# Hybrid streaming encoder step, attention stage: a quarter of the full weight units split on GpSimd, causal mask on VectorE, reciprocals turned in 32 by 32 blocks, half of w_out split on GpSimd

## The reference

```python
s = jnp.einsum('bqhd,bkhd->bhqk', qi, k, preferred_element_type=jnp.float32) * sc
s = s + (Fi[:, :, :, None] - Ft[:, :, None, :])
s = jnp.where(kpos[None, :] <= qpos[:, None], s, -jnp.inf)
pr = jax.nn.softmax(s, axis=-1)
return jnp.einsum('bhqk,bkhd->bqhd', pr.astype(v.dtype), v)
...
z = jnp.concatenate([attn * jax.nn.silu(ag), pool * jax.nn.silu(pg)], axis=-1)
return x + gate[:, None, :] * (z @ w_out)
```

## Time and profile before

| | us |
|---|---|
| median of three runs | 1268.88 (1265.78 to 1271.44) |
| profiled execution, its time | 1271.73 |
| its span, first to last instruction | 1269.9 |
| mean granted TensorE clock | 0.989 of full speed |

### The profile page before, as it was taken

One profiled execution on the slowest core, in us unless ns is written; L12 is line 12 of the kernel. 1 busy time (PEld: TensorE's weight loads), 2 busy tenths in 40 slices (PEclk: granted clock), 3 DMA queues, 4 the chain that ended last, 5 costly groups with the idle time before them and its releaser, 6 DMA issues. The chain is left out here.

```text
span 1269.9 us, 19390 instructions
## 1 busy us (share of the span) xinstructions
PE 1231.5 (97%) x7023; PEld 1029.5 (81%) x7023; DVE 714.3 (56%) x1974; ACT 565.9 (45%) x1163; POOL 185.3 (15%) x193
## 2 busy tenths in 40 slices
PE   5899999999999999999999999999999998999997
PEld 1799988888888888888878788877877876888886
DVE  1756433333564121110059899999999999444444
ACT  3756321222121111211158788887888878111111
POOL 1433301010010100101000051032013106100000
PEclk9899999999999999999989999999999999999999
DMA  9856454022122344347174759849777875666663
GB/s 365 321 174 189 144 152 141 34 69 83 36 85 69 135 147 137 112 128 182 53 166 41 148 95 162 120 103 178 100 136 137 90 188 148 190 203 199 199 199 100
DMA packets 162037, 179.52 MB, mean 141 GB/s; under 512 B 34789, under 2 KB 124265, under 8 KB 157782
## 3 DMA queue, kind: packets, MB, share of 16 engines
q1 hardware_dynamic: 157174, 161.24, 51.2%
q10 hardware_dynamic: 4768, 17.04, 4.1%
HBM read 111.55 MB, written 66.69 MB: 140 GB/s over the span
## 5 line engine op out<-in xcount | busy, mean ns | idle before, releaser
L617 PE MATMUL prj_acc<-prj_hhi,til_whi 128*128 128x512 f32 (+1 forms) x800 | 285.9, 357 | 0.0
L618 PE MATMUL prj_acc<-prj_hhi,til_wlo 128*128 128x512 f32 (+1 forms) x800 | 284.8, 356 | 0.0
L619 PE MATMUL prj_acc<-prj_hlo,til_whi 128*128 128x512 f32 (+1 forms) x800 | 283.7, 355 | 0.0
L1603 DVE TENSOR_SCALAR_CACHE_REDUCE att_wts<-att_sps 128x512 f32<-128x512 f32 (+4 forms) x328 | 186.7, 596 | 92.3 <-PE att_sps L1468 90.9
L1613 DVE TENSOR_TENSOR att_wlo<-att_tps,att_whi 128x512 fp32r<-128x512 f32 (+1 forms) x336 | 183.5, 584 | 17.9 <-ACT att_whi L1547 17.1
L1547 ACT ACTIVATE att_whi<-att_tps 128x512 fp32r<-128x512 f32 (+1 forms) x336 | 160.8, 516 | 53.1 <-PE att_tps L1481 28.5
L1541 ACT ACTIVATE att_wts<-att_wts,att_nm 128x1024 f32<-128x1024 f32 (+8 forms) x200 | 175.2, 880 | 16.6 <-DVE att_nm L1608 14.3
L617 PEld LDWEIGHTS prj_acc<-prj_hhi,til_whi 128*128 128x128 f32 x800 | 150.5, 188 | 22.0
L619 PEld LDWEIGHTS prj_acc<-prj_hlo,til_whi 128*128 128x128 f32 x800 | 150.5, 188 | 21.6
L618 PEld LDWEIGHTS prj_acc<-prj_hhi,til_wlo 128*128 128x128 f32 x800 | 150.6, 188 | 21.0
L1481 PE MATMUL att_tps<-keep_ident,att_wts 128*128 128x128 f32 x1088 | 159.9, 277 | 7.5 <-DVE att_wlo L1613 6.8
(11 more groups left out here) (202 smaller groups left out, 1861.4 us busy)
## 6 DMA issues: line engine op xcount, KB each, us to landing
til_wraw<-in_w_in SPq DMA_DIRECT2D x20, 512.0 KB, 4.1
scratch_v<-val_vs SPq DMA_DIRECT2D x17, 512.0 KB, 4.7
val_xt<-in_x_prompt ACTq DMA_DIRECT2D x16, 512.0 KB, 4.5
ini_al<-in_w_ada SPq DMA_DIRECT2D x8, 1024.0 KB, 15.7
zin_zh<-scratch_z SPq DMA_DIRECT2D x16, 512.0 KB, 4.3
zin_zl<-scratch_z SPq DMA_DIRECT2D x16, 512.0 KB, 5.8
zin_xr<-in_x_prompt SPq DMA_DIRECT2D x16, 512.0 KB, 5.5
out_y_prompt<-zin_o ACTq DMA_DIRECT2D x15, 512.0 KB, 2.7
```

Source lines behind the costliest of these rows:

```text
L617: pe.matmul(out, w[0][:, k, :], hhi[:, k, cs], start=(k == 0), stop=False)
L618: pe.matmul(out, w[1][:, k, :], hhi[:, k, cs], start=False, stop=False)
L619: mm = pe.matmul(out, w[0][:, k, :], hlo[:, k, cs], start=False, stop=(k == KT - 1))
L1603: dve.tensor_scalar(weights(st, x.row, x.w0, x.n), sps[x.i % S_RING][0:x.m, 0:x.n], 1.0, None, ALU.mult, ALU.max, accum_out=top[0:x.m, e, ...
```

## The change

- **Split on GpSimd.** `POOL_UNITS` are the units with index 3 modulo 4 that are 512 wide, not of the sample rows, and not in the last step: 49 of 336. ScalarE copies their bank to one of two plain float32 buffers `wf`; GpSimd copies that to `whi` and subtracts for `wlo`. The next turn into that bank waits for ScalarE alone. Their value matmuls wait for GpSimd.
- **Order.** GpSimd becomes a fourth engine of `Plan`, with its gate passes as separate items ranked behind the splits. Value is ranked ahead of score on TensorE, except that a score comes first when no copied bank is outstanding (`rank`).
- **Gates.** For pairs 0 to 2 `gate_in` is issued one step later, after the next step's `rec_out`; for the last pair it stays.
- **Reciprocals.** They go to a 128x32 tile, which VectorE transposes in 32 by 32 blocks; four DMAs store rows of 128 bytes.
- **Mask.** A float32 mask of 576 columns is made by GpSimd after the norm stage. The third score matmul is gone; VectorE adds the mask in the pass that copies the diagonal block.
- **w_out.** Slices 4 to 7 are subtracted by GpSimd.

```diff
 DEC = 64
 PAST = 128
+MASK_COLS = DEC + 4 * P
...
-MASKED = -1e30
+MASKED, LOWEST = -1e30, -3e38
...
-            pool.memset(keep["mask"][:, :], 0.0).then_inc(const, 1)
             pool.memset(one[:, :], 1.0).then_inc(const, 1)
-            pool.wait_ge(const, 3)
+            pool.wait_ge(const, 2)
...
-            pool.affine_select(out=keep["mask"][:, :], in_=keep["mask"][:, :], compare_op=ALU.is_ge, fill=MASKED,
-                               base=0, pattern=[[-1, P]], channel_multiplier=1).then_inc(const, 1)
-
             pool.affine_select(out=tri[:, :], in_=one[:, :], compare_op=ALU.is_ge, fill=0.0,
                                base=0, pattern=[[1, P]], channel_multiplier=-1).then_inc(const, 1)
-            pool.wait_ge(const, 6)
-            pool.tensor_copy(keep["identb"][:, :], ident[:, :]).then_inc(const, 1)
...
+            pool.wait_ge(sq, NT)
+            pool.memset(keep["mask"][:, :], 0.0).then_inc(masked, 1)
+            pool.wait_ge(masked, 1)
+            for c0, n in ((0, DEC), (DEC + 3 * P, P)):
+                pool.affine_select(out=keep["mask"][:, c0:c0 + n], in_=keep["mask"][:, c0:c0 + n], compare_op=ALU.is_ge, fill=MASKED,
+                                   base=0, pattern=[[-1, n]], channel_multiplier=1).then_inc(masked, 1)
...
 S_RING, T_RING, W_RING, O_RING = 3, 3, 6, 2
+F_UNITS = 2
+W_DVE = KT // 2
+POOL_UNITS = [u.i for u in UNITS if u.i % 4 == 3 and not u.dec and not u.skip and u.step.index < len(STEPS) - 1]
+GATED = [out for out in OUTS if out.step.e == 1]
+GATE_LAG = 6000
+def gate_step(st):
+    return st.index + (st.head < HEADS - 1)
...
+def dve_units(i):
+    return i + 1 - sum(j <= i for j in POOL_UNITS)
...
-    PRIORITY = {"PE": ("turn", "score", "value"), "ACT": ("out", "high", "exp", "w_high"), "DVE": ("low", "add", "score", "den", "w_low")}
+    PRIORITY = {"PE": ("turn", "value", "score"), "ACT": ("out", "high", "exp", "w_high"), "DVE": ("low", "add", "score", "den", "w_low"),
+                "POOL": ("p_high", "p_low", "g_lo", "g_z", "g_hi", "g_mul", "w_plow")}
...
+    def turned(self, i):
+        return self.at("high" if i in POOL_UNITS else "low", i)
+    def halved(self, i):
+        return self.at("p_low" if i in POOL_UNITS else "low", i)
...
-            return max(at("exp", LAST_PIECE[x.i]), at("low", x.i - T_RING))
+            return max(at("exp", LAST_PIECE[x.i]), self.turned(x.i - T_RING))
         if kind == "value":
-            return max(at("low", x.i), at("add", x.out.i - O_RING) if x.first else 0, self.arrived(x, x.c))
+            return max(self.halved(x.i), at("add", x.out.i - O_RING) if x.first else 0, self.arrived(x, x.c))
...
+            if x.i in POOL_UNITS:
+                r = POOL_UNITS.index(x.i)
+                return max(at("turn", x.i), at("p_low", POOL_UNITS[r - F_UNITS]) if r >= F_UNITS else 0)
...
+        if kind == "p_high":
+            return max(at("high", x.i), at("value", x.i - W_RING))
+        if kind == "g_mul":
+            return max(at("add", x.i), at("den", gate_step(x.step)) + GATE_LAG)
+        if kind in ("p_low", "g_hi", "g_z", "g_lo"):
+            return at({"p_low": "p_high", "g_hi": "g_mul", "g_z": "g_hi", "g_lo": "g_z"}[kind], x.i)
...
-            mask = 50 if kind == "score" and x.last else 0
-            return 24 + 6 * x.n // 7 + mask + (80 if self.short else 0), 200
+            return 24 + 9 * x.n // 10 + (80 if self.short else 0), 200
+        if kind == "w_plow":
+            return 2400, 150
+        if engine == "POOL":
+            return (650 if kind == "p_high" else 1300 if kind == "p_low" else 30 + 5 * x.width // 2), 130
...
+    def rank(self, engine, kind, x, t):
+        if engine != "PE" or kind != "score":
+            return self.PRIORITY[engine].index(kind)
+        waiting = sum(self.at("copied", i) > t for i in range(max(0, x.i - S_RING), x.i))
+        return -1 if waiting < 1 else 0.5 if waiting < 2 else 2
...
-                    key = (begin, self.PRIORITY[engine].index(kind))
+                    key = (begin, self.rank(engine, kind, table[n], begin))
...
-                self.short = kind == "turn" or (kind == "score" and x.last)
+                self.short = kind == "turn"
...
+def mask_of(x):
+    at = 0 if x.row == NQ else DEC + 3 * P - x.mask0
+    return slice(at, at + x.n)
...
+        wf = [s.sb(f"wf{n}", [P, 512]) for n in range(F_UNITS)]
...
-        rec = s.sb("rec", [P, 2, NR])
+        rec = s.sb("rec", [P, NG, 32])
+        rec_t = s.sb("rec_t", [P, NG, 32])
...
+        def rec_at(col):
+            return 8 * P if col == SEQ else col + P * (col >= 8 * P)
         def rec_out(sp, st):
-            sp.wait_ge(rec_ok, st.index + 1)
-            h, e, r = st.head, st.e, st.rows
-            sp.dma_start(dram["rden"][h, P * r.start:P * r.stop].rearrange("(t p) -> p t", p=P),
-                         rec[:, e, r], allow_slow_non_contiguous=True).then_inc(rd_out[e], 16)
-            if 0 in st.groups:
-                sp.dma_start(dram["rden"][h, SEQ:T].rearrange("(p t) -> p t", t=1), rec[0:DEC, e, NQ:NR]).then_inc(rd_out[e], 16)
+            sp.wait_ge(rect_ok, st.index + 1)
+            h, e, r, first = st.head, st.e, st.rows, 0 in st.groups
+            at = rec_at(P * r.start)
+            for b in range(4):
+                n = r.stop - r.start + (first and b < 2)
+                dst = dram["rden"][h, at:at + P * n].rearrange("(t b c) -> b t c", b=4, c=32)[b]
+                sp.dma_start(dst, rec_t[32 * b:32 * b + n, st.index % NG, :]).then_inc(rd_out[st.index % NG], 16)
...
-            sp.wait_ge(rd_out[0], 16 * NRD * (st.pair + 1))
-            sp.wait_ge(rd_out[1], recs(st))
+            sp.wait_ge(rd_out[st.index % NG], 128 * (st.pair + 1))
...
+                if st.index and STEPS[st.index - 1].e == 1 and gate_step(STEPS[st.index - 1]) == st.index:
+                    gate_in(sp, STEPS[st.index - 1])
...
-                if st.e == 1:
+                if st.e == 1 and gate_step(st) == st.index:
                     gate_in(sp, st)
...
-                    mm = pe.matmul(bank[0:x.m, 0:x.n], qb[e][:, q], kb[e][:, k], start=False, stop=not x.last)
-                    if x.last:
-                        mm = pe.matmul(bank[0:x.m, x.mask0:x.mask0 + x.m], keep["identb"][0:x.m, 0:x.m],
-                                       keep["mask"][0:x.m, 0:x.m], start=False, stop=True)
+                    mm = pe.matmul(bank[0:x.m, 0:x.n], qb[e][:, q], kb[e][:, k], start=False, stop=True)
...
-                    if x.i >= T_RING:
-                        pe.wait_ge(lo_ok, x.i - T_RING + 1)
+                    if x.i - T_RING in POOL_UNITS:
+                        pe.wait_ge(hi_ok, x.i - T_RING + 1)
+                    elif x.i >= T_RING:
+                        pe.wait_ge(lo_ok, dve_units(x.i - T_RING))
...
-                    pe.wait_ge(lo_ok, x.i + 1)
+                    if x.i in POOL_UNITS:
+                        pe.wait_ge(p_ok, POOL_UNITS.index(x.i) + 1)
+                    else:
+                        pe.wait_ge(lo_ok, dve_units(x.i))
...
-                    if i == 0:
+                    if i == 0 and k < W_DVE:
                         pe.wait_ge(w_lo, k + 1)
+                    elif i == 0:
+                        pe.wait_ge(w_plo, k - W_DVE + 1)
...
+                elif kind == "high" and x.i in POOL_UNITS:
+                    r = POOL_UNITS.index(x.i)
+                    act.wait_ge(t_full, x.i + 1)
+                    if r >= F_UNITS:
+                        act.wait_ge(p_ok, r - F_UNITS + 1)
+                    act.activation(wf[r % F_UNITS][:, :], tps[x.i % T_RING][:, :], ACT.Copy).then_inc(hi_ok, 1)
...
-                    dve.tensor_scalar(weights(st, x.row, x.w0, x.n), sps[x.i % S_RING][0:x.m, 0:x.n],
-                                      1.0, None, ALU.mult, ALU.max,
-                                      accum_out=top[0:x.m, e, x.row, x.b:x.b + 1]).then_inc(s_free, 1)
-                    if x.last:
+                    w, src, most = weights(st, x.row, x.w0, x.n), sps[x.i % S_RING][0:x.m, 0:x.n], top[0:x.m, e, x.row, x.b:x.b + 1]
+                    if not x.last:
+                        dve.tensor_scalar(w, src, 1.0, None, ALU.mult, ALU.max, accum_out=most).then_inc(s_free, 1)
+                    else:
+                        dve.tensor_tensor_reduce(w, src, keep["mask"][0:x.m, mask_of(x)], 1.0, LOWEST, ALU.add, ALU.max,
+                                                 accum_out=most).then_inc(s_free, 1)
...
-                    if x.index % NG == 0 and x.head >= 2:
-                        dve.wait_ge(rd_out[e], 16 * NRD * (x.head // 2))
                     if x.index % NG >= 1:
                         dve.tensor_tensor(den[:, e, r, 0], den[:, e, r, 0], den[:, e, r, 1], ALU.add).then_inc(den_sum, 1)
                         dve.wait_ge(den_sum, 2 * x.head + x.index % NG)
-                    else:
-                        dve.reciprocal(rec[0:DEC, e, NQ:NR], den[0:DEC, e, NQ:NR, 0])
```

(37 more changed lines are left out.)

74 lines of the change are left out of this document (39 added, 35 removed).

## The result

The changed kernel takes **1277.07 us** (median of 4 runs, 1276.51 to 1277.87) against 1268.84 for the kernel before on the same chip: a ratio of 1.0064, 95% interval 1.0038 to 1.0090. It is slower by 8 us, where 1252 us was predicted and 1266 was the upper end of the range. The profiled execution took 1276.51 us (span 1274.8), against 1271.73.

What follows compares the result with a forecast made beforehand. TensorE was taken as the tighter engine, with VectorE nearly as full. Eight heads gain 21 us and the stage's end 4, less 7 for GpSimd's lateness and 1 for additions: 17 us off 1268.9, 1252 us, range 1236 to 1266.

Steps and rivals of the forecast that it cites:

- Loads: Attention, per head: TensorE falls from 49.0 to 47.1 us, VectorE from 48.6 to about 45.7 us.
- `den` additions: VectorE in attention: 16 small additions may wait for GpSimd passes; 5 us worked out, 1 us taken in the sum.
- rival 3: Diagonal blocks on VectorE: mask costs a second pass or port waiting, making VectorE the tighter engine; 1267 us, chance 0.08.
- GpSimd's lateness, +7 us: Attention gates: late gates hold splits queued behind them and so TensorE's value matmuls; 7 us, bounds 0 and 30.
- Rival 4: GpSimd gate passes waiting for `rb` hold splits and values; kernel slower, put at 1280 us, chance 0.10.
- the two marks that the text gave (10 and 30): TensorE's summed waits for GpSimd: not above 10 us if the forecast holds, above 30 us for Rival 4.
- TensorE is the tighter engine: Attention: a head takes TensorE's 47.1 us plus 2.7 us, 49.8 in all; 21 us less over eight heads.
- Two engines bind each other: Attention before the change: TensorE and VectorE bind through three-bank rings, 3.4 and 3.8 us spare per head, neither alone the limit.
- The order rule "at zero": TensorE's order, value ahead of score: no net changes of kind, with 3 changes (0.25 us) per head either way.
- Reciprocals, "nothing is gained by itself": SyncE's 62.1 us of store waits are hidden; shorter rows gain nothing, unshortened ones make the last pair's gates 8 us late.
- End of the stage, -4 us: End of attention: four w_out slices leave VectorE, gaining 4 us, bounds 8 and -2.
- Rival 2: Attention: late value matmuls of every fourth unit empty the rings; only 8 to 12 us faster, 1260 us, chance 0.10.

Runs made afterwards that it cites:

- e1: The changed kernel with q and k loads of heads 3, 5 and 7 issued a step later, behind the gate loads: 1258.8 us, 0.9921 of the kernel before.
- e2: The changed kernel, DMAs unchanged, plan's lag raised for the last gate of pairs 0 to 2, so two splits precede it: 1262.4 us, 0.9933 of before.
- e4: The kernel before with only the mask moved to VectorE's pass, no third score matmul: 1.0028 of the kernel before.
- e16: e4 with the new TensorE order rule (turn, value, score) and nothing else: 1.0094 of the kernel before.
- e11: e9 with the mask back on TensorE: 1.0038 of the kernel before.
- e10: e9 with TensorE's old order rule (turn, score, value): 0.9967 of the kernel before.
- e3: The changed kernel without any split on GpSimd: 1.0085 of the kernel before.
- e13: e9 with reciprocals stored from their columns in 4-byte rows as before, no transposes: 1.0429 of the kernel before.
- e9: e1 with the gates' real lags given to the plan, the program's DMAs the same: 0.9916 of the kernel before.
- e17: e13 with the plan given lags of 14, 24 and 28 us, and 8 behind the gate two before: 1.0278 of the kernel before.
- e7: e1 with all of w_out back on VectorE: 0.9931 of the kernel before.

## Why the prediction was wrong, point by point

The kernel is 25 us slower than forecast. 11 of them are the lateness of GpSimd, 18 us instead of 7, and without them the time would lie inside the range (e1, 1258.8). The other 14 are a gain of the relieved engines that was put too high (e1 against 1245).

- **Loads: right.** TensorE -15 us (forecast 8 x 1.9), -14.9 by the estimate above, which other groupings put at 7 to 20; mask pass 684 ns; copy 0.61 us (forecast 0.7); VectorE kept 175 subtractions of 512 columns (170 of them in the window shown). Of 16 `den` additions one took 1.27 us and the median was 163 ns: 1 us in all, as was put in the sum, and not the 5 us worked out before it. A dear mask pass (rival 3) is out.
- **GpSimd's lateness, +7 us: the step that failed first.** It measured 17 us in e2 and 18 in e1. The step took the median landing of 4.0 us, "0.7 late for each of 15 gates", and named the 18.4 us beside it without asking which gate that was. It is the last gate of each of the first three pairs: six of the 40 loads of the earlier trace rows took 15.7 to 18.4 us, and all six are of these gates, behind the q and k loads in SyncE's list. In GpSimd's list it stands right before the next head's first splits. A lateness of 30 us spread over 20 gates was multiplied by a quarter; in truth three gates, each 11 us later than the plan had it, met a split every time. Rival 4 named place and mechanism, with "loads in flight, landing up to 18.4 us", and had a chance of 0.10. Its form was different: not 20 gates at 3 to 4 us but three at 11.5, 4.5 us of each reaching TensorE. The sum of TensorE's waits for GpSimd, 14.4 us, lies between the two marks that the text gave (10 and 30).
- **"TensorE is the tighter engine", 2.7 us a head: right in part.** This is the second step that failed, and the larger one. Without the collision the forecast would have been 1245 us; e1 gives 1258.8. By the estimate of the load its time beyond it is 41 us against 39 before, where the step expected 5.6 less; of e1's 12.6 us of gain in the stage up to 5 can be the clock, which is at half for 3.4 us of its stage against 13.7 before. TensorE's relief alone gave nothing (e4), and without splits the order rule cost 8 us (e16 against e4). With splits both pay, 15 and 6 us (e11, e10). "Two engines bind each other" stood in the first part; the sum then went by one of them. The gain is of the parts together: the mask is worth 15 us beside the splits and nothing alone. Why the time beyond the load did not fall stays open. The range of this term was also added up wrongly: 1.7 to 3.4 us kept beyond 47.1 gives 15 to 29 us for eight heads, not 14 to 26.
- **The order rule "at zero": wrong in size, both ways.** -6 us beside splits, +8 without, and part of both can be the clock.
- **Reciprocals, "nothing is gained by itself": right and misleading.** Alone nothing (e3 equals e16), but the splits stand on them: with the 4-byte stores 65 us are lost (e13 against e9), 46 of them still with the right lags in the plan (e17), where the text had the last pair's gates 8 us late. The waits of 62.1 us in the earlier trace rows were free only while GpSimd had nothing else to do; the text said so, and stopped at the step of room.
- **End of the stage, -4 us: not shown.** e7 with all of `w_out` on VectorE is 1.4 us above e1, within the noise; TensorE's waits there are 3.3 us in three in e7 and 3.0 in e1. From the last reciprocals (1070.5) to the output projection (1085.7) it is 15 us, under the 28 that were given as a mark; it was 20 before (1060.8 to 1080.8), but it is 16 in e7 too, so the moved slices are not the cause.
- **Rival 2** (relief given back) was a mark of 1260 us; e1 lies there, by another way: not that late values empty the rings, as TensorE waits only 1.2 us for splits in e1, but that the time beyond the load stayed.

The sum in place of the text's: -21 and -4 became -12.6 for the stage of e1; +7 became +18; together +5.5 for the stage, and the profiled execution is 4.8 us longer.

## What to carry to other kernels

When free time of an engine with an ordered list is filled with work on the critical path, every wait that was harmless in that list becomes a wait of the path: go through them one by one, by the longest and not by the median, and ask what will stand behind each. A plan needs the landing times that the trace shows, buffers that come free late included; a variant measured with a wrong plan tells about the plan. Where two engines bind each other, the price of one part is only valid beside the others: measure it both ways. And before a difference of a few us is given to a change of order, compare the granted clock of the two traces.
